# The key norms with tokens on partitions, and two projections and the RG-LRU beside the first RWKV tile

## What is computed

```python
q, k, v, g_a, x_b, g_b, c_cols, g_c = jnp.split(proj, split_idx, axis=-1)
y_a = _swa_sinks(q, k, v, attn_sinks[l])
y_b = _rg_lru(x_b, conv_w[l], conv_b[l], lru_wa[l], ...)
y_c, v_own = _rwkv7(c_cols, rwkv_mu[l], rwkv_w0[l], ...)
y = jnp.concatenate([y_a * silu(g_a), y_b * silu(g_b), y_c * silu(g_c)], axis=-1)
```

## Time and profile before

| | |
|---|---|
| Median of 3 runs | 2325.89 us (2322.83 to 2327.24) |
| Profiled execution | 2324.63 us, span 2322.8 us |
| PE busy | 2115.5 us, 91% of the span |
| DVE busy | 825.8 us, 36% |
| ACT busy | 557.4 us, 24% |
| Preparation | from about 345 to 412 us of the span |
| The eight tiles | from 412 us on |

### The profile page before, as it was taken

One profiled execution on the slowest core, in us unless ns is written; L12 is line 12 of the kernel. 1 busy time (PEld: TensorE's weight loads), 2 busy tenths in 40 slices (PEclk: granted clock), 3 DMA queues, 4 the chain that ended last, 5 costly groups with the idle time before them and its releaser, 6 DMA issues. The chain is left out here.

```text
span 2322.8 us, 27359 instructions
## 1 busy us (share of the span) xinstructions
PE 2115.5 (91%) x10876; PEld 1221.1 (53%) x10876; DVE 825.8 (36%) x1853; ACT 557.4 (24%) x1349; POOL 198.8 (9%) x297
## 2 busy tenths in 40 slices
PE   8999999799989579999978999999999849999991
PEld 4545554686438344444435657767764324444440
DVE  1106549664435421111124533443431141111115
ACT  1013235232113111112213333333321101111112
POOL 0000002011522010000001000000000000000003
PEclk9999999899989779999998999999999969999996
DMA  3501000200211359999963000000100068999966
GB/s 127 217 23 37 19 2 3 75 4 3 83 49 47 165 204 366 394 397 369 369 240 109 11 0 1 1 1 1 73 13 37 36 253 305 366 369 367 369 268 245
DMA packets 46199, 349.30 MB, mean 150 GB/s; under 512 B 6256, under 2 KB 6576, under 8 KB 36208
## 3 DMA queue, kind: packets, MB, share of 16 engines
q1 hardware_dynamic: 32176, 296.97, 32.7%
q0 software_dynamic: 13888, 50.47, 6.2%
HBM read 292.82 MB, written 54.59 MB: 150 GB/s over the span
## 5 line engine op out<-in xcount | busy, mean ns | idle before, releaser
L202 PE MATMUL psum<-arena 128*128 128x512 f32 (+9 forms) x9328 | 1957.1, 386 | 108.1 <-DVE arena L1968 25.9
L202 PEld LDWEIGHTS psum<-arena 128*128 128x128 f32 (+3 forms) x9328 | 1048.4, 171 | 947.4 <-issue 835.2
L2099 DVE TENSOR_TENSOR arena<-psum,arena 128x256 f32<-128x256 f32 x64 | 27.2, 425 | 540.4 <-ACT arena L2143 540.4
L2179 POOL DMA_INDIRECT arena<-xn_rows,arena x64 | 60.1, 939 | 817.9 <-PE psum L2066 588.7
L2143 ACT ACTIVATE arena<-psum 128x256 f32<-128x256 f32 x64 | 24.7, 386 | 400.9 <-PE psum L202 400.9
L1520 ACT ACTIVATE arena<-arena 128x1024 f32<-128x1024 f32 x43 | 45.4, 1056 | 251.4 <-DVE arena L2834 101.6
L2747 ACT ACTIVATE arena<-psum,arena 128x1024 f32<-128x1024 f32 (+8 forms) x72 | 50.2, 699 | 188.7 <-DVE arena L2783 188.7
L2136 ACT ACTIVATE arena<-psum 128x512 f32<-128x512 f32 x64 | 38.2, 597 | 185.5 <-PE psum L202 185.5
L2066 PE MATMUL psum<-arena 128*128 128x128 f32 x512 | 68.2, 278 | 11.0 <-DMA arena<-xn_rows,arena 11.0
L1221 ACT ACTIVATE arena<-psum 128x256 f32<-128x256 f32 (+3 forms) x128 | 43.9, 355 | 104.0 <-PE psum L202 93.1
L2166 DVE COPY arena<-psum 128x512 f32<-128x512 f32 x64 | 44.3, 692 | 61.0 <-PE psum L202 61.0
(11 more groups left out here) (289 smaller groups left out, 1282.2 us busy)
## 6 DMA issues: line engine op xcount, KB each, us to landing
arena<-in_w_exp SPq DMA_DIRECT2D x64, 3072.0 KB, 11.7
expert_rows<-arena SPq DMA_DIRECT2D x80, 512.0 KB, 3.8
arena<-in_x SPq DMA_DIRECT2D x16, 512.0 KB, 4.4
xn_rows<-arena SPq DMA_DIRECT2D x16, 512.0 KB, 2.6
arena<-in_w_out SPq DMA_DIRECT2D x8, 512.0 KB, 7.9
arena<-in_w_o SPq DMA_DIRECT2D x1, 4096.0 KB, 12.1
out<-arena SPq DMA_DIRECT2D x8, 512.0 KB, 5.2
arena<-in_rows SPq DMA_DIRECT2D x6, 512.0 KB, 6.3
```

What stands on the lines that cost most here:

```text
L202: return e.matmul(out, lhsT, rhs, start=start, stop=stop, skip_group_check=True)
L2179: e.indirect_dma_start(out=xe, out_offset=None, in_=xn_dram[:, :], in_offset=bass.IndirectOffsetOnAxis(idx.bitcast(I32)[:, block:block + 1 ...
```

## The change

**Key norms.** The squared keys are now the stationary operand, and two columns of the ones matrix the moving one: 16 small products ("kn") give the sums with tokens on partitions, 32 numbers a partition. The root and the reciprocal run on 128 x 32. ACT spreads the result to 128 x 1,024 per half (`kk_b`, which lies in `Em`), 16 products with the identity ("kk") bring it back to channels on partitions, and DVE multiplies kk by it out of PSUM. ACT squares the keys with their scale directly, and it makes the convolution's first tap.

**Order.** ACT's exponentials move ahead of the LRU gates. The rk products move up between the LRU products of j = 0 and j = 1. `left[1]` stands ahead of kk.

**Beside tile 0.** `left[4]` and `left[5]` leave the preparation. PE does two of their products ahead of each of steps 1 to 8 of tile 0; ACT and DVE drain them in step 9. The RG-LRU's DVE operations stand one to a step, the scans and the last multiplications in tiles 1 and 2. Tile 1's buffers move to where x and the sigmoids lay.

```diff
-        def pe_project(e, n):
+        def pe_project(e, n, part=range(KD)):
...
+            if part[0] == 0:
...
+                wait_all(e, pj.free(n))
...
+            for k in part:
...
+            if part[-1] == KD - 1:
+                i.then_inc(*pj.fill(n))
...
+        kk_dev, kk_r = take(4 * NT), take(4 * NT)
+        kk_b = Em.rearrange("p a b -> p (a b)").rearrange("p (a b) -> p a b", b=HD)
...
+        lru_t = psum[:, 512 * 4:512 * 6]
...
+        order = [("kn", "S")] + [(("wa",) + x, "S") for x in DECAY] + [(("kk", j, hf), "V") for j in range(2) for hf in range(2)]
+        for j in range(2):
+            order += [(("lru",) + x, "S") for x in LRU_MM if x[1] == j]
+            if j == 0:
+                order += [(("rk", jj, hf), "V") for jj in range(2) for hf in range(2)]
...
+        LATE = left[4:]
+        LATE_AT = {step: (LATE[(step - 1) // 4], range(2 * ((step - 1) % 4), 2 * ((step - 1) % 4) + 2)) for step in range(1, 9)}
...
-            for j in range(2):
-                e.wait_ge(*kk_sq.at(j + 1))
-                for hf in range(2):
-                    key = ("kk", j, hf)
-                    wait_all(e, pr_.free(key))
-                    mm(e, pr_.bank[key], pair_ones, Lc[:, j, half_cols(hf)], True, True).then_inc(*pr_.fill(key))
+
+            e.wait_ge(*kk_sq.at(2))
+            wait_all(e, pr_.free("kn"))
+            for t in range(NT):
+                for j in range(2):
+                    m = mm(e, pr_.bank["kn"][:, 4 * t + 2 * j:4 * t + 2 * j + 2], Lc[:, j, P * t:P * (t + 1)], pair_ones[:, 0:P:HD], True, True)
+            m.then_inc(*pr_.fill("kn"))
...
+            pe_project(e, left[1])
+
+            e.wait_ge(*kk_wide.at(2))
             for j in range(2):
-                pe_project(e, left[1 + j])
+                for hf in range(2):
+                    key = ("kk", j, hf)
+                    wait_all(e, pr_.free(key))
+                    for u in range(4):
+                        c = 4 * (4 * hf + u) + 2 * j
+                        m = mm(e, four(pr_.bank[key])[:, u, :], kk_b[:, c:c + 2, :].rearrange("p a b -> p (a b)"), ident, True, True)
+                    m.then_inc(*pr_.fill(key))
+            for j in range(2):
+                if j:
+                    pe_project(e, left[2])
...
+                if j == 0:
+                    for jj in range(2):
+                        e.wait_ge(*rk_in.at(jj + 1))
+                        for hf in range(2):
+                            key = ("rk", jj, hf)
+                            wait_all(e, pr_.free(key))
+                            mm(e, pr_.bank[key], pair_ones, tmp[jj][:, half_cols(hf)], True, True).then_inc(*pr_.fill(key))
...
             for j in range(2):
-                e.wait_ge(*kk_raw.at(j + 1))
-                e.activation(Lc[:, j, :], kk[:, j, :], ACT.Square).then_inc(*kk_sq.up())
+                e.activation(Lc[:, j, :], R[2 + j], ACT.Square, scale=col("k_k", j)).then_inc(*kk_sq.up())
+
+            e.wait_ge(*pj.full(last_of["vwa"]))
+            for j in range(2):
+                e.wait_ge(*pj.empty(last_half["xb", j]))
+                e.activation(xc[:, j, :], xb[:, j, 0:T], ACT.Identity, bias=col("conv_b", j), scale=col("conv_w", 4 * j)).then_inc(*conv_in.up())
             act_project(e, left[0])
-            for j in range(2):
-                for hf in range(2):
...
+            e.wait_ge(*kk_in.at(1))
+            for c in (0, 2 * NT):
+                e.activation(kk_b[:, c:c + 2 * NT, :], bc_last(kk_r[:, c:c + 2 * NT], HD), ACT.Copy, bias=0.0).then_inc(*kk_wide.up())
+            for j in range(2):
+                e.wait_ge(*scanned.at(j + 1))
+                e.activation(Ep[:, j, :], Lc[:, j, :], ACT.Exp, scale=-EXP_HALF).then_inc(*exped.up())
+
+                e.wait_ge(*pr_.full(("kk", 1, 1)))
+                e.activation(Em[:, j, :], Lc[:, j, :], ACT.Exp, scale=EXP_HALF).then_inc(*exped.up())
+            for j in range(2):
+                e.wait_ge(*to_exp.at(j + 1))
+                e.activation(sgm[:, j, :], sgm[:, j, :], ACT.Exp, scale=-EXP_HALF).then_inc(*exped.up())
...
+            e.wait_ge(*pr_.empty("kn"))
+            e.reciprocal(kk_r, kk_dev).then_inc(*kk_in.up())
...
-                e.reciprocal(tmp[j], tmp[j]).then_inc(*V.up())
-                e.wait_ge(*V.last())
-                e.tensor_tensor(kk[:, j, :], kk[:, j, :], tmp[j], ALU.mult).then_inc(*V.up())
...
+                    kc = kk[:, j, half_cols(hf)]
+                    e.wait_ge(*pr_.full(key))
+                    e.tensor_tensor(kc, pr_.bank[key], kc, ALU.mult).then_inc(*pr_.drain(key, "V"))
+            dve_project(e, left[1])
...
+        def dve_bonus(e, j):
+            for hf in range(2):
+                key = ("rk", j, hf)
+                e.wait_ge(*pr_.full(key))
+                e.tensor_tensor(bonus[:, j, half_cols(hf)], pr_.bank[key], R[4 + j][:, half_cols(hf)], ALU.mult).then_inc(*pr_.drain(key, "V"))
...
+        LRU_ACT = {(0, 4): ("sqrt", 0), (0, 6): ("sqrt", 1)}
+        LRU_DVE = {(0, 0): ("gate", 0), (0, 1): ("gate", 1), (0, 2): ("square", 0), (0, 3): ("rest", 0), (0, 4): ("square", 1), (0, 5): ("rest", 1),
+                   (0, 6): ("input", 0), (0, 8): ("input", 1), (1, 2): ("scan", 0), (1, 5): ("scan", 1), (1, 9): ("out", 0), (2, 2): ("out", 1)}
...
-        after_prep = pr_.totals + pj.totals + [(prep_v.sem, 2), (exped.sem, 6), (lru_a.sem, 2), (rk_in.sem, 2), m_lru]
+        after_prep = pr_.totals + [pj.empty(left[3]), (prep_v.sem, 2), (exped.sem, 6), (rk_in.sem, 2), m_lru]
...
+                if i == 0 and s in LATE_AT:
+                    pe_project(e, *LATE_AT[s])
+                if (i, s) == (0, 10):
+
+                    wait_all(e, pj.totals)
...
+                if (i, s) == (0, 9):
+                    for n in LATE:
+                        act_project(e, n)
...
+                if (i, s) == (0, 9):
+                    for n in LATE:
+                        dve_project(e, n)
+
+                    e.memset(STt[:, 0], 0.0).then_inc(*states.up())
```

More of the change, by code:

```diff
@@ L325, in build @@
         st = [[take(AH) for _ in range(6)] for _ in range(3)]
+        base_sums = top[0]
         tmp = [take(T) for _ in range(2)]
@@ L739, in act_prep @@
             for j in range(2):
-                e.wait_ge(*kk_raw.at(j + 1))
-                e.activation(Lc[:, j, :], kk[:, j, :], ACT.Square).then_inc(*kk_sq.up())
-            act_project(e, left[0])
[L743 to L747, removed]
+                e.activation(Lc[:, j, :], R[2 + j], ACT.Square, scale=col("k_k", j)).then_inc(*kk_sq.up())
[3 more added lines that the diff above has]
+                e.activation(xc[:, j, :], xb[:, j, 0:T], ACT.Identity, bias=col("conv_b", j), scale=col("conv_w", 4 * j)).then_inc(*conv_in.up())
+            act_project(e, left[0])
+            e.wait_ge(*pr_.full("kn"))
+            e.activation(kk_dev, pr_.bank["kn"][:, 0:4 * NT], ACT.Sqrt, bias=eps_kk).then_inc(*pr_.drain("kn", "S"))
             for j, what, hf in DECAY:
@@ L762, in act_prep @@
             for j in range(2):
[L763 to L769, removed]
                 e.wait_ge(*pr_.empty(("lru", "x", 1, 1)))
@@ L825, in dve_prep @@
                 e.tensor_tensor(kk[:, j, :], kk[:, j, :], sgm[:, j, :], ALU.mult).then_inc(*prep_v.up())
[L826 to L834, removed]
-                    dve_project(e, left[5])
@@ L837, in act_lru @@
-        def act_lru(e, step):
-            if step in (5, 6):
-                j = step - 5
+            dve_bonus(e, 1)
+            dve_project(e, left[2])
+            dve_project(e, left[3])
+        def dve_bonus(e, j):
+            for hf in range(2):
+                key = ("rk", j, hf)
+                e.wait_ge(*pr_.full(key))
+                e.tensor_tensor(bonus[:, j, half_cols(hf)], pr_.bank[key], R[4 + j][:, half_cols(hf)], ALU.mult).then_inc(*pr_.drain(key, "V"))
+        LRU_ACT = {(0, 4): ("sqrt", 0), (0, 6): ("sqrt", 1)}
@@ L847, in dve_lru @@
                 e.wait_ge(*pr_.empty(("lru", "x", 1, 1)))
                 e.tensor_tensor(ib[:, j, :], ib[:, j, :], xc[:, j, :], ALU.mult).then_inc(*V.up())
-            elif step in (2, 3):
-                j = step - 2
+            elif what == "square":
                 e.wait_ge(*lru_a.at(j + 1))
-                e.tensor_tensor(lru_t[:, j, :], ra[:, j, :], ra[:, j, :], ALU.mult).then_inc(*V.up())
+                if j:
+                    e.wait_ge(*lru_q.at(1))
+                e.tensor_tensor(lru_t, ra[:, j, :], ra[:, j, :], ALU.mult).then_inc(*V.up())
+            elif what == "rest":
@@ L853, in dve_lru @@
                 e.wait_ge(*V.last())
-                e.scalar_tensor_tensor(out=q_[:, j, :], in0=lru_t[:, j, :], scalar=1.0, in1=q_[:, j, :], op0=ALU.add,
+                e.scalar_tensor_tensor(out=q_[:, j, :], in0=lru_t, scalar=1.0, in1=q_[:, j, :], op0=ALU.add,
                                        op1=ALU.mult).then_inc(*lru_q.up())
-            elif step in (7, 8):
-                j = step - 7
```

(11 more changed lines are left out.)

90 lines of the change are left out of this document (38 added, 52 removed).

## The result

The changed kernel is slower: 2330.05 us (median of 22 runs, 2325.28 to 2337.43) against 2324.06 for the kernel before, ratio 1.0025 with a 95% interval of 1.0017 to 1.0033, some 6 us. I had forecast 7 us less, in a range of 2311.5 to 2328, so both the way and the range were missed.

A forecast was written before the change was run, and what follows sets the result against it. PE, busy for 91% of the span, was taken as the bound. Preparation -12.3, tile 0's front +4.9, tile 1 0 and tile 2 +0.5 sum to -6.9 us: 2319.0 against the median of 2325.89, range 2311.5 to 2328.

The forecast's parts named there:

- kn's price: In the preparation on PE: 16 new products of 2 columns, 32 records, taken at 3.0 us, between 1.5 and 4.7.
- the full clock behind it: In the preparation behind kn: decay products at 4.9 us as before, to 360.0, then left[1] to 366.9.
- The preparation: Stretch from left[0] to tile 0's start: tile 0 starts at 399.6 instead of 411.9, -12.3 us.
- clock 1.00 stands in every stretch with a full PE: Argument for a rival of more gain, 2314 us, chance 0.2, with the clock holding at full in tile 1.
- Rival (d): New waits set PE back to half clock and tile 0's front pays in full: slower, 2332 us, chance 0.1.
- the three new waits: PE pauses of 2.2 us before rk, 2.3 before tile 0 and 3 before tile 1.
- The bounds under my forecast: kn -1.5 to +1.7, wait before rk -1.5 to +1, tile 1 -1.9 to +1.5, tile 2 -0.5 to +2.2: about 2315 to 2322.
- The front: Tile 0's front with the late projections: tile 1 starts 26.7 us after tile 0 instead of 21.8, +4.9 us.
- Rival (b): Late projections not hidden in tile 0's front, which takes 35.5 us: 2327.8 us, chance 0.17.
- Tile 1: Scans cost DVE 1.1 us more, the clock should hold better: 19.1 us taken, change 0, bounds 17.4 to 20.6.
- the wait ahead of the third rk product: In the preparation: PE stands 2.2 us for the first LRU product's bank, which ACT drains only after the Exps.
- the signs set down for a wrong prediction: Tile 0's front over 30 us, or its clock under 0.8; or tile 0 starting after 404.

The follow-up runs named there:

- e1: The changed kernel with kn's 16 products moving 128 columns instead of 2; 2324.74 us, ratio 1.0004 to the kernel before.
- e11: Preparation's queues as in the kernel before, all six projections in it; only the RG-LRU's DVE and ACT operations at the changed steps; 2321.81 us, ratio 0.9988.
- e2: The changed kernel with left[4] and left[5] put back into the preparation, behind left[3]; 2329.25 us, ratio 1.0020 to the kernel before.
- e4: The changed kernel with one product of eight left of each late projection, at steps 4 and 8; 2317.81 us, ratio 0.9969 to the kernel before.
- e7: e1 with the RG-LRU's scans and one last multiplication in steps 7 and 8 of tile 0 instead of in tile 1; 2318.78 us, ratio 0.9984.
- e5: e1 with left[2] done between the LRU products of j = 0 and the rk products, instead of behind rk; 2321.16 us, ratio 0.9986.
- e6: e1 with left[4] drained in step 7 of tile 0 and left[5] in step 9, instead of both in step 9; 2322.80 us, ratio 0.9990.
- e10: e1 with the late projections in two blocks of eight products, ahead of steps 1 and 5 of tile 0; 2327.76 us, ratio 1.0018.
- e12: The kernel of e8 run once more, for its interval; 2314.26 us, ratio 0.9959 to the kernel before.
- e8: The changed kernel with the changes of e1, e5, e6 and e7 together; 2315.12 us, ratio 0.9961 to the kernel before.
- e9: e1 with the late projections in four blocks of four products, ahead of steps 1, 3, 5 and 7 of tile 0; 2324.93 us, ratio 1.0004.

## Why the prediction was wrong

**The step that failed first** is kn's price and the full clock behind it. I took 3.0 us from the records' length, and the record count and length were near (32, whose starts lie within 3.4 us):

```profile
L202 PE MATMUL psum<-arena 128*128 128x2 f32 x32 | 3.6, 249 | 0.0
```

The Trainium skill ("TensorE: Matmul & The Clock Gate", section on LDWEIGHTS) makes it 3.4 as an estimate, and the trace agrees. But I walked the rest of the preparation at full clock, since PE had no pause in it, and named the clock only for waits. The clock fell for 10.2 us with no wait ahead of it, while PE went from kn to the decay products and left[1]. The preparation missed by 6.4 us, and e1 gets 5.2 of them back: 3.5 ahead of the third rk product and 1.7 of the fall behind the wait for it. The 1.2 left are about what the wide kn takes over my 3.0 (4.2). Why the clock falls behind narrow products is not shown, only that it does.

My argument that "clock 1.00 stands in every stretch with a full PE" was read from one execution: e11, with the same queue in the preparation as the kernel before, has 6.8 us of full PE at 0.50. In the sum's terms, I let some 21 us at half clock shrink to 3.4, and 20.4 were there.

Rival (d), 2332 us, comes nearest to the measured 2330.05, and that is luck. It asked for some 23 us more at half clock, and there were none more. It had falls behind the three new waits, and three of 3.4 us stand there; the longest stands behind kn, which no rival named. The bounds under my forecast also add up to 2313.6 to 2325.4, not to 2315 to 2322; 2330.05 is outside either.

**The front: +9.2 for +4.9.** The walk was right that PE would bound it and that the drain of the late projections would come behind step 9: from ACT's last copy (431.12) to tile 1's first mask (434.98) are 3.9 us, 4.0 in the sum. What was short is the middle, 4.4 us (27.1 from the first product at 403.98 to that copy, 22.7 in the sum). Its parts: 1.7 us of clock, by the fall at 405.4; and the blocks. By the records' starts a block reaches from the last small record at 409.97 over the four wide ones (410.12 to 411.51) to the next small one at 412.03, 2.06 us where I had 1.72: eight times 0.3 is 2.4 us. Together they are 4.1.

e2 and e11 show further that the front's 21.1 us were no measure of room: 4.7 of them were the RG-LRU's pairs, which the new table takes out anyway, and the chain left is 16.4 us. In e4, 12.0 us of PE cost 11.0. Rival (b), not hidden, had the cost of the projections nearly right, but added it to the old 21.8 us: it made the front 35.5 us, and measured from the first product it is 31.0, between (b) and my 26.7.

**Tile 1: +1.7 for 0.** I added up DVE's spare time in a tile (5.6 us) against 1.1 us more work. The spare time is not where the scans stand. A scan of 2.28 us ahead of L1403 or L1414 delays the state chain: PE waits 2.19 and 1.94 us there. e7 took the scans out and tile 1 lost 3.2 us. The better clock in tile 1 (0.92 for 0.80), which I had set against the scans, did come.

**Right**: the wait ahead of the third rk product (2.2 forecast, 2.35 measured), its cause and its worth (e5: 1.9 us for a wait of 1.70, and no other pause in its place); left[3]'s late sigmoid, 2.5 us of PE pause before tile 0 (2.3 forecast); the switch of tables at 1.3 us. Two of the signs set down for a wrong prediction appeared: a front of over 30 us, and, at 404.0, the edge of the one for tile 0's start.

On the switch, the changed kernel agrees with the earlier trace rows and not with the 2.66 us of the Trainium skill ("ScalarE: Activation LUTs", What ACT_TABLE_LOAD costs):

```profile
378.02 1.28 ACT L363 ACT_TABLE_LOAD   x1
379.32 0.60 ACT L363 ACTIVATE arena<-psum 128x512 f32<-128x512 f32 x1
379.81 2.42 ACT L798 ACTIVATE arena<-psum,arena 128x512 f32<-128x512 f32 x4
```

## What to carry to other kernels

Products with few columns can have a second price: here PE's clock fell behind a row of them in all three profiles that have it. Where weights nearly set the pace anyway, wide operands cost little (0.8 us here, for about 5 gained). One profile in which the clock held is no proof that it holds: look at a second one of the same queue before counting on it. Count a stretch's room from its chain without the work that the change also moves, and place filler by the pause it goes into: the sum of an engine's idle time over a tile says nothing on an operation that stands ahead of the chain. And when two parts each lose alone, look for the piece that gains alone; here it was a table of steps.

## What the runs showed of the hardware

The same 32 weight loads with 2 moving columns start within 3.4 us and with 128 within 4.2. Behind the first the granted clock fell to 1.2 GHz for 10.2 us of full PE in three profiles of three; behind the second it did not, in eight of eight. In two profiles with neither it fell for 3.4 and 6.8 us around the decay products.

A block of four records of 128 x 128 with 512 columns between small products of 64 x 64 takes some 0.3 us over its own 1.72: the first comes 0.15 us behind the last small record, the second 0.1 later than its spacing, and the next small one another 0.1 later.

A pause of PE of 2.5 us ahead of tile 0 was followed by a fall of 3.4 us within two us in the changed kernel, e4, e6, e7, e10 and e12, and by none in the front of e1, e5, e8 and e9. In tile 1 the clock varies as well: e5 differs from e1 only in the place of left[2] in the preparation, yet has three falls in tile 1 where e1 has the clock at 0.92, and takes 25.6 us instead of 20.7; e9 took 25.6 too. I have not found what decides it; single profiles of these kernels were therefore read by stretch, and the verdicts by the medians.
